# The order of the heads in the attention of tiles 1 to 5 of a hybrid decoder step, and where its scores and turned probabilities lie

## What is computed

```
z   = rmsnorm(x) @ w_in                      # queries, keys, values of two head groups
o_a = attention(q_a, k_a, v_a) in a window of 128, with sinks   # 8 heads, 2 of keys ("near")
o_b = combination of three dilated windows (1, 4, 16)            # 8 heads ("far")
x   = x + [norm(o_a), norm(o_b)] @ w_out
h   = rmsnorm(x)
x   = x + PEER(h)      # per token 8 heads x 16 experts of 16384:
                       # top-16 by product keys, gelu(h . u[e]) * gate, sum of v[e]
y   = rmsnorm(x)
```

## Time and profile before

| | |
|---|---|
| median of 3 runs | 3300.21 us (3298.2 to 3306.2) |
| the profiled execution | 3299.21 us, span 3297.4 us |
| mean granted TensorE clock | 0.876 |
| busy: TensorE, VectorE, ScalarE, POOL | 76%, 77%, 56%, 40% |
| DMA traffic | 1262.28 MB, mean 383 GB/s |
| attention of tile 1 | about 206 to 350 us |
| tile 2 | 364 to 475 us |
| tile 3 | 763 to 945 us |
| tile 4 | 957 to 1097 us |
| tile 5 | 1392 to 1675 us |
| tiles 6 and 7 | 1690 to 1850 us, 2186 to 2470 us |

### The profile page before, as it was taken

How to read it: one execution, slowest core, us unless ns; L and a number is a source line. 1 busy time by engine, 2 the same in 40 slices (tenths; PEclk the granted TensorE clock), 3 DMA queues, 4 the chain that set the end, 5 groups by cost and what they waited for, 6 DMA issues and landing times.

```text
span 3297.4 us, 34302 instructions
## 1 busy us (share of the span) xinstructions
PE 2499.9 (76%) x7082; PEld 1252.6 (38%) x7082; DVE 2522.7 (77%) x6081; ACT 1830.5 (56%) x5867; POOL 1321.9 (40%) x1044
## 2 busy tenths in 40 slices
PE   7968757888876679878787789968775577776665
PEld 4534435444433344434334343334332223432221
DVE  1268888888977878889877878888976657888665
ACT  1246664456666545566676645556675445556554
POOL 0023343344433434445444434444454234445553
PEclk8989958998977789999897789989998789889887
DMA  9979988999989899999999999999999989999997
GB/s 329 353 312 389 397 356 319 394 408 397 383 338 369 345 384 417 408 409 410 405 414 371 361 384 414 403 391 411 407 422 373 349 334 403 407 395 407 410 421 312
DMA packets 191355, 1262.28 MB, mean 383 GB/s; under 512 B 24848, under 2 KB 32872, under 8 KB 46736
## 3 DMA queue, kind: packets, MB, share of 16 engines
q0 software_dynamic: 149760, 1086.39, 81.7%
q1 hardware_dynamic: 41384, 173.70, 14.2%
HBM read 1251.24 MB, written 43.37 MB: 393 GB/s over the span
## 4 chain that ended last, share of the span: by engine, by line
DMA 32%; DVE 23%; PE 21%; issue 8%; ACT 5%; SPq 4%; DVEq 4%; POOL 3%; ACTq 1%; POOLq 0%
DMA uv_ring<-in_peer_uv,idx 29%; PE acc L1715 10%; DVE uv_ring L2386 9%; DVE accs L2393 4%; POOL uv_ring L1419 3%; PE pS L1478 2%; PE pS L1597 2%; PE pA L1620 2%; SPq L1277 1%; ACT bent L1995 1%; PE acc L1478 1%; SPq L1312 1%; DMA S<-in_cache_swa 1%; ACT diag L1771 1%; ACT wv L1998 1%
## 5 line engine op out<-in xcount | busy, mean ns | idle before, releaser
L1419 POOL DMA_INDIRECT uv_ring<-in_peer_uv,idx x1024 | 1305.7, 1275 | 1932.4 <-PE acc L1715 1428.5
L1715 PE MATMUL acc<-uv_ring,diag 128*128 128x512 f32 x2552 | 1405.3, 690 | 498.7 <-ACT diag L1771 487.7
L2386 DVE SCALAR_TENSOR_TENSOR uv_ring<-uv_ring,hb 128x1024 f32<-128x1024 f32 x1032 | 1240.9, 1220 | 370.9 <-DMA uv_ring<-in_peer_uv,idx 348.6
L1715 PEld LDWEIGHTS acc<-uv_ring,diag 128*128 128x128 f32 x2552 | 511.7, 215 | 1211.9 <-ACT diag L1771 723.8
L1991 ACT ACTIVATE cube<-dots 128x1 f32<-128x1 f32 x1032 | 204.2, 198 | 962.3 <-DVE uv_ring L2386 959.2
L2393 DVE SCALAR_TENSOR_TENSOR accs<-uv_ring,wv,accs 128x1024 f32<-128x1024 f32 x386 | 494.1, 1280 | 21.1 <-ACT wv L1998 19.2
L1995 ACT ACTIVATE bent<-dots,cube 128x1 f32<-128x1 f32 x1032 | 399.1, 387 | 74.0 <-issue 2.8
L1771 ACT ACTIVATE diag<-diag,wv 128x128 f32<-128x128 f32 x638 | 256.2, 402 | 51.9 <-issue 1.8
L1998 ACT ACTIVATE wv<-bent,dots 128x1 f32<-128x1 f32 x638 | 246.9, 387 | 45.0 <-issue 0.7
L1771 ACT ACTIVATE diag<-idn,gates 128x128 f32<-128x128 f32 x638 | 238.0, 387 | 1.7 <-DVE gates L2278 1.7
L1620 PE MATMUL pA<-T,wbuf 128*128 128x256 f32 (+1 forms) x1024 | 224.0, 375 | 18.4 <-issue 10.5
(11 more groups left out here) (273 smaller groups left out, 2212.1 us busy)
## 6 DMA issues: line engine op xcount, KB each, us to landing
wbuf<-in_w_q SPq DMA_DIRECT2D x40, 1024.0 KB
out_dil_s<-in_cache_dil SPq DMA_DIRECT2D x8, 4092.0 KB
wbuf<-in_w_in SPq DMA_DIRECT2D x26, 1024.0 KB
wbuf<-in_w_out SPq DMA_DIRECT2D x20, 1024.0 KB
uv_ring<-in_peer_uv,idx POOLq DMA_INDIRECT x1024
uv_ring<-in_w_in SPq DMA_DIRECT2D x6, 1024.0 KB, 16.8
keysT<-in_keys SPq DMA_DIRECT2D x40, 128.0 KB
T<-in_xT_all SPq DMA_DIRECT2D x8, 512.0 KB, 13.1
```

What stands on the lines that cost most here:

```text
L1419: pool.indirect_dma_start(uv_ring[:, entry % RING, :], None, peer_uv, bass.IndirectOffsetOnAxis(rows, 0))\
L1715: m = pe.matmul(acc[0:R, side * 512:(side + 1) * 512], w, uv_ring[:, entry % RING, D + side * 512:D + (side + 1) * 512], start=first, stop ...
L2386: dve.scalar_tensor_tensor(row, row, GELU_C, h, ALU.mult, ALU.mult, accum_out=dots[:, e % RING:e % RING + 1]).then_inc(u_dot, 1)
```

## The change

For tiles 1 to 5 (`piped`) the stages of a tile are listed in another order: the scores of head a + 1 stand ahead of the turned probabilities of head a, and the maxima and exponentials of head a + 1 ahead of the values of head a. The near scores go to `pS[768:1024]`, the near turned probabilities to `pT` behind the far ones, so `pM` holds only the values; `PT` keeps the near blocks right behind the far ones, and ScalarE copies all blocks in pieces of four. The scores no longer wait for the previous head's output; the values do now, and in each tile the first head's transposes. The small tiles of maxima and denominators alternate between two sets. The planner's durations are as before; its stage order and inputs follow the new one.

```diff
+def piped(t):
+    return 1 <= t <= 5
...
 def attention_stages(t):
...
+    elif piped(t):
+        out += [("s", t, 0), ("sm", t, 0), ("se", t, 0)]
+        for a in range(HEADS):
+            more = a + 1 < HEADS
+            out += [("s", t, a + 1)] if more else []
+            out += [("p", t, a), ("pe", t, a)]
+            out += [("sm", t, a + 1), ("se", t, a + 1)] if more else []
+            out += [("v", t, a), ("vd", t, a), ("vo", t, a)]
     else:
...
 def inputs_of(n, stages, places):
...
+    pair = 2 if kind == "vd" and piped(a) else two
...
     if kind == "s":
-        return (last("zv") + last("ze") if b == 0 else []) + items("sm", two) + items("vo", two) + last("ox")
+        return (last("zv") + last("ze") if b == 0 else []) + items("sm", two) + (items("vo", two) if not piped(a) else []) + last("ox")
...
     if kind == "p":
-        return at("se", a, b) + items("pe", two) + (items("vo", 2) if a == 0 else []) + (last("zv") + last("hv") + last("ng") if b == 0 else [])
+        return at("se", a, b) + items("pe", two) + (items("vo", 2) if a == 0 else []) + (last("vo") if piped(a) and b == 0 else []) + (last("zv") + last("hv") + last("ng") if b == 0 else [])
...
     if kind == "vd":
-        return at("se", a, b) + items("vo", two)
+        return at("se", a, b) + items("vo", pair)
...
@@ scores(t, a) @@
                 need(pe, a_max, A)
-                need(pe, a_o, A)
+                if not piped(t):
+                    need(pe, a_o, A)
                 q = queries_of(t)
+                near = pS[:, 768:1024] if piped(t) else pM[:, 0:256]
...
-                    m = pe.matmul(pM[:, 0:256], q[rows, p, :],
+                    m = pe.matmul(near, q[rows, p, :],
...
@@ prob_transposes(t, a) @@
                 need(pe, a_te, A)
-                for k in range(blocks_of(t)):
+                n = blocks_of(t)
+                if piped(t) and a == 0:
+                    need(pe, a_o, A)
+                near = pT[:, n * P:(n + 2) * P] if piped(t) else pM[:, 256:512]
+                for k in range(n):
...
-                    m = pe.transpose(pM[:, 256 + k * P:256 + (k + 1) * P], S[:, D + k * P:D + (k + 1) * P], idn[:, :])
+                    m = pe.transpose(near[:, k * P:(k + 1) * P], S[:, D + k * P:D + (k + 1) * P], idn[:, :])
...
@@ values(t, a) @@
+                n = blocks_of(t)
+                need(pe, a_o, A)
...
-                    m = pe.matmul(pM[:, 64:128], PT[:, 8 + k, :], vA[:, (t - 1 + k) % NEAR, par * HD:(par + 1) * HD],
+                    m = pe.matmul(pM[:, 64:128], PT[:, (n if piped(t) else 8) + k, :], vA[:, (t - 1 + k) % NEAR, par * HD:(par + 1) * HD],
...
@@ softmax(t, a), head_out(t, a), maxima(t, a) @@
-                b = par if t == 0 else 0
+                b = par if t == 0 or piped(t) else 0
...
@@ probs_out(t, a) @@
-                for b0, b1 in halves_of(blocks_of(t)):
-                    copy(PT[:, b0:b1, :], pT[:, b0 * P:b1 * P].rearrange("p (b n) -> p b n", b=b1 - b0))
+                for b0, b1 in halves_of(blocks_of(t) + (2 if piped(t) else 0)):
+                    m = copy(PT[:, b0:b1, :], pT[:, b0 * P:b1 * P].rearrange("p (b n) -> p b n", b=b1 - b0))
+                if piped(t):
+                    m.then_inc(a_te, 1)
+                    return
                 copy(PT[:, 8:10, :], pM[:, 256:512].rearrange("p (b n) -> p b n", b=2)).then_inc(a_te, 1)
...
@@ maxima(t, a) @@
-                    dve.tensor_tensor_reduce(S[:, D:D + 256], pM[:, 0:256], maskA[:, :], 0.125, NEG,
+                    near = pS[:, 768:1024] if piped(t) else pM[:, 0:256]
+                    dve.tensor_tensor_reduce(S[:, D:D + 256], near, maskA[:, :], 0.125, NEG,
...
@@ denominators(t, a) @@
-                b = a % 2 if t == 0 else 0
+                b = a % 2 if t == 0 or piped(t) else 0
                 dve.wait_ge(a_exp, A + 1)
-                need(dve, a_o, A - 1 if t == 0 else A)
+                need(dve, a_o, A - 1 if t == 0 or piped(t) else A)
```

More of the change, by code:

```diff
@@ L1536, in scores @@
                     for k in range(2):
-                        m = pe.matmul(pM[:, k * P:(k + 1) * P], q[rows, p, :], kTA[rows, (t - 1 + k) % NEAR, :],
+                        m = pe.matmul(near[:, k * P:(k + 1) * P], q[rows, p, :], kTA[rows, (t - 1 + k) % NEAR, :],
                                       start=True, stop=True)
@@ L1571, in values @@
                     return
-                for k in range(blocks_of(t)):
-                    pe.matmul(pM[:, 0:64], PT[:, k, :], VB[:, k, cols], start=(k == 0), stop=(k == blocks_of(t) - 1))
+                n = blocks_of(t)
+                need(pe, a_o, A)
+                for k in range(n):
+                    pe.matmul(pM[:, 0:64], PT[:, k, :], VB[:, k, cols], start=(k == 0), stop=(k == n - 1))
                 for k in range(2):
-                    m = pe.matmul(pM[:, 64:128], PT[:, 8 + k, :], vA[:, (t - 1 + k) % NEAR, par * HD:(par + 1) * HD],
+                    m = pe.matmul(pM[:, 64:128], PT[:, (n if piped(t) else 8) + k, :], vA[:, (t - 1 + k) % NEAR, par * HD:(par + 1) * HD],
                                   start=(k == 0), stop=(k == 1))
```

## The result

The changed kernel takes 3277.49 us (median of 5 runs, 3262.57 to 3286.49) against 3300.21 us; the ratio is 0.9935, with a 95% interval of 0.9908 to 0.9962. So the gain is about 21 us by the ratio (22.7 us between the medians). It was forecast as 29.5 us, and 3277 lies in the range of 3235 to 3308 us. The profiled execution took 3279.36 us, 19.9 us less than that of before.

The account below looks back on a forecast made before the run. The prediction took the DMA transfers to be near their limit, with only their pauses, about 4% of the span, to win. Savings in five tiles' attention summed to 29.5 us: 3299.2 - 29.5 = 3269.7, said as 3270 us, range 3235 to 3308.

Parts of the forecast that it names:

- the waits for exponentials and copy: Sign of being right: TensorE's waits for these average no more than 1 us in tiles 2 and 4.
- the shorter tiles: Sign of being right: each changed tile's attention gets shorter or has fewer urgent stages.
- the share of 0.98 in tiles 2 and 4: Sign of being right: the DMA share during attention of these tiles reaches 0.98 or more.
- rival 2: Whole kernel: the pause only moves to another place, leaving 3299 us, within 10 us of it; chance 0.19.
- The chain: Attention heads of tiles 1 to 5: pace-setting handovers take at most 6.8 us in place of 16.3.
- What it gives: Pauses in attention of tiles 1 to 5: 1.5, 8, 5, 14 and 1 us saved, sum 29.5 us.
- Later stretches: Output projections and rankings after tiles 2 and 4: pauses of 18.8 and 8.2 us, gain taken as 0.
- rival 3: Attention and later stretches: planner lag is worked off afterwards, so 58.3 us are gained, 3241 us; chance 0.19.
- Tiles 1, 3 and 5: Attention of these tiles: gains of 1.5, 5 and 1 us, from pauses of 11.5, 10.9 and 2.8 us.
- Copies, banks, values' wait: Attention: fewer ScalarE copies, new banks and values waiting for the previous head's output each change the time by 0.
- Rival 4: Attention: VectorE stalls before maxima, waiting for turned probabilities; over about 2 us delays dots; 3319 us, chance 0.15.
- The clock: TensorE's granted clock: low level alone costs nothing here, so the sum has no term for it.

Follow-up runs that it names:

- E9: Kernel before with the planner's bias for TensorE at -1.5 instead of -1.0 and the new order in tiles 2 and 4 only: 0.9935 of the kernel before.
- e10: Kernel before with the planner's bias for TensorE at -1.5 and the new order in tiles 1, 3 and 5 only: 0.9941 of the kernel before.
- e1: Changed kernel with each pick weighed by the engine that weighed it in the kernel before (646 picks on TensorE): 1.0010 of the kernel before, 3303 us.
- e3: Changed kernel's banks, copies and small-tile pairs, but with lists, waits and plan of the kernel before: 0.9994 of the kernel before, 3300 us.
- the four pairs: Old and new order each planned at TensorE biases -0.5, -1.0, -1.5 and -2.0: new over old 0.9955, 0.9935, 0.9893 and 0.9813.
- e5: Kernel before, old order, with the planner's bias for TensorE at -0.5 instead of -1.0 (627 picks there): 0.9946 of the kernel before.
- e7: Kernel before, old order, with the planner's bias for TensorE at -1.5 instead of -1.0 (724 picks there): 0.9989 of the kernel before.
- e4: Kernel before with the new order in tiles 2 and 4 only, bias unchanged: 0.9992 of the kernel before, 3295 us.
- e12: Changed kernel with the planner's bias for TensorE at -2.0 instead of -1.0 (833 picks there): 0.9875 of the kernel before, 3250.98 us.

## Why the prediction was right, and where it was not

The sign and the size of the total held, and TensorE's waits inside attention did halve. Where the pauses would go, and so the way from the waits to the time, did not hold. Of the signs that the prediction named, the waits for exponentials and copy (0.8 and 2.7 us over the 8 heads of tile 2, 3.3 and 5.0 us in tile 4) and the shorter tiles came true, but the share of 0.98 in tiles 2 and 4 did not: it is 0.90 and 0.91, which the prediction had called a sign of rival 2. Step by step:

- **The chain.** The 6.8 us were the whole ring of a head, from turned to turned by way of maxima and exponentials. It is 11.0 us in the head shown, and the pace of the heads went only from 17.0 to 13.2 us in tile 4 (eight heads' maxima from 966.25 to 1084.91 us before, from 950.61 to 1043.26 us after). The chain has room that picks and scores fill.
- **What it gives.** This is the step that failed: the pauses were taken off the tiles' own stretches, 8 us in tile 2 and 14 in tile 4. The trace shows 0.5 and 8.1 us there, 6.7 over all five (tile 5's pause even grew by 5.2 us). The hole of the earlier trace rows went, but the denser attention has others.
- **Later stretches.** Taken as 0, they gave 4.8 and 1.1 us in one execution of each kernel, against 5.4 us for a new hole between tiles 3 and 4; and tile 6, which should have read as before, gave 7.3 us. So the total came out near by luck: too much was expected of the tiles and too little of the rest. By the fetches the stretch from 206 to 593 us, where tile 2's 8 us were expected, brought 2 us. What was said for rival 3, base work that is ahead instead of urgent, may be part of it; its 58 us of gain are far off.
- **Tiles 1, 3 and 5.** 7.5 of 29.5 us were put to them. E9 and e10 give them nearly half, on one plan each.
- **Left out.** I wrote that new plans could move a hole, but didn't see that the planner would turn shorter waits into 50 more picks on TensorE. With the shares of before forced on it (e1) the order gives nothing. The base stages' order was costed as if the picks' share stayed.
- **Copies, banks, values' wait: 0.** e3 confirms it, within 0.2%.
- **Rival 4.** VectorE does not stand before the maxima. The group in tile 4 of the changed kernel:

```profile
L2177 DVE CUSTOM_DVE_ANT_0 S<-pS,maskB 128x640 f32<-128x640 f32 x8 | 6.6, 824 | 3.1 <-PE pT L1578 2.1
```

Its idle time of 3.1 us for 8 heads (1.9 us before) is 0.4 us per head, far from the 2 us per head from which it would decide. What took its place is TensorE's wait for the maxima, 23.3 us, smaller than the 27.0 us for the output that it replaced.
- **Rival 2** missed the time, but its reasons were partly met: the hole at 924 to 940 us is new, the share in tile 4 is still 0.91, and the old order reaches 0.9946 by another plan. The change at one bias could not have told a gain of the order from chance of the plan; the four pairs do.
- **The clock.** I gave it no term. With all but equal picks on TensorE it rises from 0.897 to 0.912 and 0.919 as none, two and all five tiles get the new order. The Trainium skill, "TensorE: Matmul & The Clock Gate" (loop structure), has it that a long wait between matmuls lets the clock drop; these traces agree in direction, with 126.4, 82.0 and 69.2 us of waits inside attention. The time does not follow the clock alone: e5 is faster at 0.880 (0.9946) than e7 at 0.900 (0.9989). How much of the gain is the clock's was not tried. The same page's case in which double-buffering PSUM gave no further gain (HAM oscillation) agrees with e3, where the other banks alone gave 0.9994; a gain came only with another order.

Open: how much of each pair's distance is order on the engines and how much the share, since no kernel holds the share fixed in a plan made for it; by which stretches and waits the new order's plans gain; why the old order is good at -0.5; and where the bias has its optimum in the new order.

## What to carry to other kernels

Taking waits out of an engine that is not the limit need not pay: here TensorE's waits inside attention were fewer in e1 and e4 too, which gained nothing. Where a planner remakes the whole program for each edit, its own spread (1.2 points over four settings of the old order) can be larger than the edit's effect (0.65% at the setting that was forecast), so compare the edit at several settings of the planner and not at one: only so did 1.0 point between the means of the two orders come out. And a pause is not always won where the edit is. Count the stretches without gaps between them, or compare when the same transfer is issued, before saying where a gain lies.

## What was not expected of the hardware

Nothing new in kind. The transfers stay the limit throughout: with TensorE busy from 76% to 82% of the span and VectorE from 77% down to 71%, the picks' transfers hold the DMA engines for about 2694 us in the kernel before (81.7% of 3297.4) and 2684 us in e12 (82.6% of 3249.9), so most of the 47.5 us between these spans is pauses. The mean granted clock went from 0.876 in the kernel before to 0.933 in e12, where TensorE has 187 picks more.
